# A norm turned by token halves inside the first down stage of a two-block transformer kernel

## The reference

```python
def rms_norm(x, g, eps=NORM_EPS):
    x32 = x.astype(jnp.float32)
    y = x32 * lax.rsqrt(jnp.mean(x32 * x32, axis=-1, keepdims=True) + eps)
    return (y * g.astype(jnp.float32)).astype(x.dtype)

def first_block(x, ...):
    ...                                  # RWKV and differential attention
    hn = rms_norm(h, ln_ffn_pre[l])
    u = causal_dwconv(hn @ w_up[l], conv_w[l], conv_b[l])
    gate, val = jnp.split(u, 2, axis=-1)
    f = (jax.nn.gelu(gate, approximate=True) * val) @ w_down[l]
    h = h + rms_norm(f, ln_ffn_post[l])
    return h

def second_block(x, norm1, w_in, ...):
    h = rms_norm_2(x, norm1[l])
    proj = h @ w_in[l]
    ...
```

## Time and profile before

| | before |
|---|---|
| median of three runs | 2955.22 us (2954.41 to 2957.77) |
| profiled execution | 2959.0 us, span 2957.2 us |
| TensorE busy | 2835.6 us, 96% of the span |
| vector engine busy | 1848.0 us, 62% |
| ScalarE busy | 1269.7 us, 43% |
| GpSimd busy | 623.0 us, 21% |
| mean granted clock of TensorE | 0.989 of 2.4 GHz |

### The profile page before, as it was taken

The page is one execution under the profiler, slowest core; times in us unless marked ns, Lnnn a source line. Parts: engine busy times, 40 slices in busy tenths (PEclk is TensorE's granted clock), DMA queues, the critical chain, the costliest instruction groups (busy, mean ns, idle before and its releaser), DMA issues.

```text
span 2957.2 us, 47458 instructions
## 1 busy us (share of the span) xinstructions
PE 2835.6 (96%) x19678; PEld 2274.4 (77%) x19678; DVE 1848.0 (62%) x2351; ACT 1269.7 (43%) x1879; POOL 623.0 (21%) x313
## 2 busy tenths in 40 slices
PE   8999998889899999999899999999899999999999
PEld 6877777777688888788678867766578888888887
DVE  3157778852599999866685554565645766653446
ACT  4145555542554555443543433343433423333334
POOL 4310122221100000254151200000012122245443
PEclk9999999999999999999999999999899999999999
DMA  6443330002423333465544553435544344465664
GB/s 216 151 121 114 110 131 30 27 26 79 143 89 106 102 101 107 155 220 180 175 133 153 164 178 122 129 112 160 192 150 131 115 150 145 150 216 196 211 238 171
DMA packets 306280, 413.79 MB, mean 140 GB/s; under 512 B 13569, under 2 KB 189834, under 8 KB 306066
## 3 DMA queue, kind: packets, MB, share of 16 engines
q1 hardware_dynamic: 291090, 363.56, 38.6%
q10 hardware_dynamic: 14976, 47.19, 4.2%
HBM read 280.64 MB, written 130.06 MB: 139 GB/s over the span
## 4 chain that ended last, share of the span: by engine, by line
PE 80%; DVE 8%; DMA 4%; issue 3%; ACT 3%; SPq 1%; POOL 1%; DVEq 0%; ACTq 0%; POOLq 0%
PE ps L511 17%; PE ps L2767 16%; PE ps L3300 13%; PE ps L3082 10%; PE ps L2124 5%; PE ps L695 4%; PE ps L1544 4%; PE ps L2175 2%; PE ps L2194 2%; DVE cb L3385 2%; PE ps L2152 1%; PE ps L1607 1%; PE ps L2155 1%; DMA kl<-qk_lo 1%; DMA residual<-src 1%
## 5 line engine op out<-in xcount | busy, mean ns | idle before, releaser
L477 POOL TENSOR_TENSOR wl<-wraw,wh 128x1024 fp32r<-128x1024 f32 x62 | 157.4, 2538 | 1103.0 <-ACT wh L472 1093.4
L511 PE MATMUL ps<-xh,wh 128*128 128x512 f32 x752 | 237.9, 398 | 5.2 <-POOL wl L477 2.3
L511 PE MATMUL ps<-xl,wh 128*128 128x512 f32 x752 | 233.3, 392 | 0.0
L511 PE MATMUL ps<-xh,wl 128*128 128x512 f32 x752 | 232.9, 391 | 0.0
L472 ACT ACTIVATE wh<-wraw 128x1024 fp32r<-128x1024 f32 x78 | 82.4, 1056 | 266.0 <-PE ps L511 205.3
L2756 POOL TENSOR_TENSOR h_dl<-h_dr,h_dh 128x1024 fp32r<-128x1024 f32 x36 | 94.7, 2633 | 477.8 <-ACT h_dh L2738 477.6
L511 PEld LDWEIGHTS ps<-xh,wh 128*128 128x128 f32 x752 | 139.6, 189 | 46.7 <-issue 9.0
L2767 PE MATMUL ps<-h_dh,h_fh 128*128 128x512 f32 x448 | 174.8, 390 | 0.7 <-POOL h_dl L2756 0.7
L2767 PE MATMUL ps<-h_dh,h_fl 128*128 128x512 f32 x448 | 174.4, 389 | 0.0
L2767 PE MATMUL ps<-h_dl,h_fh 128*128 128x512 f32 x448 | 174.3, 389 | 0.0
L511 PEld LDWEIGHTS ps<-xl,wh 128*128 128x128 f32 x752 | 142.4, 189 | 30.3
(11 more groups left out here) (507 smaller groups left out, 7634.6 us busy)
## 6 DMA issues: line engine op xcount, KB each, us to landing
h_fr<-act_d SPq DMA_DIRECT2D x60, 512.0 KB, 3.9
act_d<-act SPq DMA_DIRECT2D x16, 1792.0 KB, 6.7
wraw<-in_w_in SPq DMA_DIRECT2D x48, 512.0 KB, 5.0
...
```

The source lines that it names most:

```text
L477: nc.gpsimd.tensor_tensor(wl[:, s, :, :], wraw[:, s, :, :], wh[:, s, :, :].bitcast(F32), ALU.subtract).then_inc(w_lo, 1)
L511: mm = nc.tensor.matmul(ps[:, bank + h, :], w, x[:, h * HALF:(h + 1) * HALF], start=start and k == 0, stop=stop and k == 2)
```

## The change

1. **Head of the down stage.** ScalarE rounds step 2 before the value tap of the last up tile instead of behind it; the vector engine takes its rest behind the gate taps instead of behind the value taps.
2. **Second half first.** Once P7 is done, tokens 512 to 1023 are complete. Their norm is done while TensorE works on P4: squares and sums among steps 36 and 37, the sum over partitions before block 0 and the spread before block 2 of step 37, then the row work tile by tile on half tiles. Steps 36 to 41 get homes of their own (`last`), outside the second half of `xh` and `xl`, so their loads wait for other things than before.
3. **Last two steps.** The operands of step 40 are rounded behind two norm tiles of the second half, those of step 41 behind three.
4. **After P4** TensorE does the second half of the first two units, with the sums and the spread of the first half's norm between, then the first half of both units with the first half's row work (`first_half_units`).
5. **Next norm's statistics.** The second half's squares are kept in `sq1` and summed between the products; root and reciprocal of that half are made in the middle of the first half's row work, and its spread at tiles 4 and 5.
6. Residual loads and stores are of half tiles; counts of the semaphores follow.

The core of the diff:

```diff
@@ scalar queue
+            down_hi_act(act, down1, 2)
             ff1_tap(act, FF_TILES - 1, "v")
-            down_hi_act(act, down1, 2)
             ff1_gelu(act, FF_TILES - 1)
-            for i in range(3, len(down1.steps)):
+            for i in range(3, LAST1 + 3):
                 down_hi_act(act, down1, i)
...
-            feature_squares_act(act, down1, 24)
-            stat_root_act(act, 3)
-            post_norm_act(act, 1, 16, 32, "norm1_2")
-
-            stat_root_act(act, 4)
+                elif i == LAST1:
+                    root_table_act(act)
+                    for m in range(4):
+                        second_half_squares_act(act, m)
+                        first_half_squares_act(act, m)
+                elif i == LAST1 + 1:
+                    for m in range(4, KT):
+                        second_half_squares_act(act, m)
+            second_half_root_act(act)
+            down_hi_act(act, down1, LAST1 + 3)
+            for kt in (0, 1):
+                second_half_act(act, kt)
+            down_hi_act(act, down1, LAST1 + 4)
+            second_half_act(act, 2)
+            down_hi_act(act, down1, LAST1 + 5)
+            for kt in (3, 4, 5):
+                second_half_act(act, kt)
+            first_half_squares_act(act, 4)
+            second_half_act(act, 6)
+            first_half_squares_act(act, 5)
+            second_half_act(act, 7)
+            for m in (6, 7):
+                first_half_squares_act(act, m)
+            stat_root_act(act, 3, HALF_BANK, FIRST_COLS)
+            post_norm_act(act, 1, 16, 32, "norm1_2", FIRST)
+
+            stat_root_act(act, 4, HALF_BANK, FIRST_COLS)
@@ vector queue
-                    if not more and x == "v":
+                    if not more and x == "g":
                         down_lo_dve(dve, down1, 2)
...
+            second_half_sum_dve(dve, KT - 1)
+            down_prepare_dve(dve, down1, LAST1 + 2)
+            second_half_reciprocal_dve(dve)
+            down_prepare_dve(dve, down1, LAST1 + 3)
+            for kt in (0, 1):
+                second_half_dve(dve, kt)
+            down_prepare_dve(dve, down1, LAST1 + 4)
+            second_half_dve(dve, 2)
+            down_prepare_dve(dve, down1, LAST1 + 5)
+            for kt in (3, 4, 5, 6):
+                second_half_dve(dve, kt)
+            feature_add(dve, down1, "P4", 0)
+            square_sum_dve(dve, 28, FIRST)
+            second_half_dve(dve, 7)
+            feature_add(dve, down1, "P4", 1)
+            square_sum_dve(dve, 29, FIRST)
+            second_half_lo_dve(dve, 7)
+            for b in (2, 3):
                 feature_add(dve, down1, "P4", b)
...
@@ tensor queue
-                down_products(pe, down1, i)
+                down_products(pe, down1, i, {0: second_half_sums_pe, 2: second_half_spread_pe} if i == LAST1 + 1 else {})
             down_last_products(pe, down1)
-            post_sums_pe(pe, 24, KT - 2)
-            spread_pe(pe, 3)
-            paced_units(pe, U_FA, 0, 16, 32, 4)
+            second_half_products(pe, 0, 1, {
+                2: lambda pe: first_half_sums_pe(pe, 24), 3: lambda pe: second_half_square_sums(pe, range(0, 4)),
+                5: first_half_spread_pe, 7: lambda pe: second_half_square_sums(pe, range(4, KT))})
+            second_half_products(pe, 1, 3, {})
+            first_half_units(pe)
@@ sync queue
+                if i == LAST1 + 3:
+                    for kt in (0, 1):
+                        second_half_loads(sp, kt)
+                elif i == LAST1 + 5:
+                    second_half_loads(sp, 2)
                 down_load(sp, down1, i)
...
+            for kt in range(3, KT):
+                second_half_loads(sp, kt)
+            post_norm_loads(sp, 1, FIRST)
@@ new functions
+        def second_half_row_dve(dve, kt):
+            s = kt % 2
+            if kt == 0:
+                h1_pe.wait(dve, "spread", 0)
+            h1_dve.done(nc.vector.tensor_tensor(y[:, kt, SECOND], y[:, kt, SECOND], ps[:, 7, :], ALU.mult), f"m{kt}")
+            h1_dve.wait(dve, f"m{kt}", 0)
+            if kt >= 2:
+                h1_dve.wait(dve, f"l{kt - 2}", 0)
+                h1_act.wait(dve, f"s{kt - 2}", 0)
+            dve.wait_ge(h_loaded[s], 16 * (4 + kt // 2 + 1))
+            dve.wait_ge(src_stored[s], 16 * ((16 + kt) // 2))
+            h1_dve.done(nc.vector.scalar_tensor_tensor(
+                out=src[:, s, SECOND], in0=y[:, kt, SECOND], scalar=col("ln_ffn_post", kt), in1=hres[:, s, SECOND],
+                op0=ALU.mult, op1=ALU.add), f"r{kt}")
+        def second_half_act(act, kt):
+            tile = src[:, kt % 2, SECOND]
+            h1_dve.wait(act, f"r{kt}", 0)
+            h1_act.done(nc.scalar.activation(xh[:, kt, SECOND], tile, ACT.Identity, scale=col("norm1_2", kt)), f"x{kt}")
+            nc.scalar.activation(y[:, kt, SECOND], tile, ACT.Identity, scale=col("norm1_2", kt))
+            h1_act.done(nc.scalar.activation(sq1[:, kt, FIRST], tile, ACT.Square), f"s{kt}")
+            act.dma_start(residual[kt][:, SECOND], tile).then_inc(src_stored[kt % 2], 16)
+        def second_half_products(pe, u, bank, after):
+            for kt in range(KT):
+                h1_dve.wait(pe, f"l{kt}", 0)
+                if kt == 0:
+                    pe.wait_ge(w_lo, U_FA + u + 1)
+                    pe.wait_ge(evac_done, U_FA + u - 1)
+                    pe.wait_ge(down_added, down_added_by(down1, "P4", bank))
+                half_tile(bank, u, kt, SECOND)
+                if kt in after:
+                    after[kt](pe)
+        def first_half_units(pe):
+            for kt in range(KT):
+                first_half_square_sum_pe(pe, 32 + kt)
+                ...
+                mm = half_tile(0, 0, kt, FIRST)
+                if 1 <= kt < KT - 1:
+                    half_tile(2, 1, kt - 1, FIRST)
+                if kt in (4, 5):
+                    next_second_half_spread_pe(pe, kt - 4)
+            mm.then_inc(mm_done, 1)
+            half_tile(2, 1, 6, FIRST)
+            next_first_half_spread_pe(pe)
+            half_tile(2, 1, 7, FIRST).then_inc(mm_done, 1)
```

295 lines of the change are left out of this document (218 added, 77 removed).

## The result

| | before | after |
|---|---|---|
| median, both in the same sessions (20 runs each) | 2957.43 us | 2961.61 us |
| ratio, 95% interval | | 1.0019, 1.0012 to 1.0026 |
| profiled execution / span | 2959.0 / 2957.2 | 2966.96 / 2965.2 |
| mean granted clock in it | 0.989 | 0.987 |

The changed kernel is slower by 0.19%, 5.6 us by the ratio and 4.2 us between the medians; 2950.3 was predicted, with 2957.0 as the upper end. The profiles are single executions: that of after (2966.96) is the second slowest of its 20 runs, so the 8.0 us between the two spans are not what the change costs.

The account below looks back on a forecast made before the run. TensorE, busy 96% of the span, was taken as the bound, so only its idle time could be won: head 2.5 plus tail 2.4 (4.6 - 0.5 - 1.7) made 4.9 us, from 2955.22 to 2950.3, range 2941.5 to 2957.0.

Parts of the forecast that it names:

- The head: Start of the down stage: step 2 begins earlier, the stall moves to step 3; 2.5 us gained after 1.7 clock loss.
- The loads there are released by TensorE, so the gain is kept: Between head and tail of the down stage: nothing there takes back the head's 2.5 us.
- The last two steps: Steps 40 and 41 of the down stage: TensorE, ready at 1436.0, waits 2.9 us for GpSimd's rest at 1438.8.
- the chain of held instructions: Tail: GpSimd's rests hold the vector engine's residual adds, delaying ScalarE's roundings and the last two steps by 2.9 us.
- Third unit at 1483.65 against 1488.26: 4.6 us gained: End of the norm turn after the down stage: third unit starts 4.6 us earlier, before deductions for round trips and clock.
- round trips: Tail: store out and load in of half tiles take 3.5 us, costing 0.15 a tile, 0.5 in the second half.
- 1.7 for the clock: Tail: pauses of 2.9, 2.5 and 3.1 us; first slow stretch hidden, one of the other two counted, 1.7 lost.
- The add of block 1: Tail, vector engine: behind tiles 3 to 7, ends at 1449.6 and frees the bank for the second half's first unit.
- the second pause: Before the second half's first products: TensorE waits 2.5 us for the add of P4 block 1.
- No holding, no clock loss: Rival: roundings of steps 39 to 41 come through and the clock stays full; 12.5 gained, 2942.7 us; chance 0.25.
- Round trips: Rival, tail: half tiles' round trips as long as whole ones', 5.4 us; 6.6 slower, 2961.8 us; chance 0.10.
- The stalls only move: Rival: head gives 1.2, both tail pauses cost slow stretches, half sums cost more; 2955.4 us; chance 0.20.

Follow-up runs that it names:

- e6: The changed kernel with all four P4 adds and squares early and tiles 0 to 4 of both second-half units first on TensorE; 2955.82 us.
- e13: The changed kernel with the four sums of P1's input made ahead of step 5's rest on the vector engine; 2961.83 us.
- e8: The changed kernel with GpSimd's rests from step 38 on cut to 64 of 512 columns, rounded weights multiplied in their place; 2959.24 us.
- e14: The changed kernel with mixed second-half units, deeper head, norm tile 2 behind step 41, and P1's sums ahead of step 5's rest; 2950.41 us.
- e3: The changed kernel with the adds of P4 blocks 0 and 1 and their squares put behind norm tile 4; 2964.48 us.
- e9: The kernel before with the head edit, and the norm's eight residual stores and loads each made as two halves, old order; 2956.20 us.

## Why the prediction was wrong

**The head.** The mechanism was right: step 2 without a pause, 3.40 us before step 3 (3.5). Step 3 came 4.75 us earlier against step 0 (4.2). The term mis-sized was the clock: 1.7 was taken, the window at 1245.47 shows 5.53 us at 0.50, 2.8 lost, as after the longer pause before; that was the lower bound of the range given. The 1.7 did not follow from its own row either: 0.69 over 4.0 us is 1.2 lost. And step 36 stands 1.43 nearer to step 0 (2.5 predicted, bounds 1.2 and 4.2). "The loads there are released by TensorE, so the gain is kept" was wrong as reasoning: the load of step 7 waits for the sums' store. It cost 0.3 in the profile of after and 3.87 in e6, but by e13 nothing in the median. In timed runs the head alone gave nothing (1.0002), so even 1.4 isn't confirmed.

**The last two steps.** P4's end was forecast to 0.2 us of what came, since its cause was: the last two steps began 25.95 us after step 36 (25.85 predicted), right behind GpSimd's rest. The wait was 1.69, not 2.9, because TensorE came there 1.3 later than forecast; the other 2.5 of the 4.2 are mostly the sum and the spreads put into step 37 (0.36 and 1.40 us, and the changes between them). e8 and e14 each take the 1.69 away, the one by shortening GpSimd's rest, the other by putting norm tile 2 behind step 41. So the chain of held instructions was right.

**The step that failed is "Third unit at 1483.65 against 1488.26: 4.6 us gained".** Counted from step 36 this is 4.3 gained (the other 0.3 lay ahead of it); the profile shows 1.7 lost, 6.0 us off. Of these the prediction had set aside 0.5 for round trips and 1.7 for the clock, which made its 2.4 for the tail; measured up to the next ring the tail lost 3.2 against the profile of before. The table gives the parts. (1) The add of block 1 came 1.85 later: five tiles took 2.04 to 2.8 us each where 1.95 stood in the sum; 0.55 and 0.78 of it are waits for round trips, for which 0.5 was taken. (2) 17.65 us instead of 15.6 for the second half's units: 1.5 of it is the clock, at 0.58 for 3.85 us behind the 4.04 us pause, and 0.6 the spread (1.40 instead of 0.8). The prediction had slow stretches behind three pauses, held the first for hidden "by the vector engine" and took one of the other two; the first didn't come, and both others did. This one wasn't hidden, as TensorE had no idle time left to give back until 1488. (3) 14.3 instead of 11.9 for the first half's units up to the last sum: six half tiles at 1.94 instead of 1.71 and one of three products, 1.6 in all, and the two parts of a spread at 0.64 each, where the sum leaves 0.3. The bounds of a half sum (0.28 and 0.57) were meant to cover this, but the sum was 0.35 as taken; it was the products beside it that cost 0.1 each way. The way from there to the third unit took 6.25, 0.3 less than forecast. (4) Behind the third unit came the slow stretch that was taken off: 3.44 us at 0.51, 1.7 lost.

**Deeper than the sizes:** the second pause was put down as a price, 2.5 us, and its cause left alone. e3 and e6 show the cause. TensorE waited for operands that it did not need to want yet; with tiles 0 to 4 of both units first, and the four adds ahead of the last tiles, 5.7 of the 6.0 us come back with no work removed. How much of it the adds and how much the products' order gives isn't shown.

**The rivals.** "No holding, no clock loss" is refuted by the held rows and the windows. "Round trips" gave 2961.8, within 0.2 of the median measured, and that is luck: it has the right sign by the wrong mechanism. The chain of after has two stores on it, of 3.69 and 4.17 us (3.5 was taken, 4.4 was the point from which it decides), the halves' median to landing was 3.6 for loads and 3.8 for stores between 1436 and 1452, and e9, with as many halves in the old order, costs nothing. The Trainium skill, "DMA: Bandwidth & Descriptors", section "Anatomy of one DMA", by which the prediction estimated 3.2 for a half tile that shares the engines, is 0.4 to 0.6 under these medians; and the 3.1 that was called agreement for a whole tile is the shortest of a set whose median is 5.0. Nearest to what happened was "The stalls only move": both pauses cost a slow stretch, and half tiles were dearer on TensorE. It gave 2955.4, and it too lacked the pace of the units and the later add.

These are the chain's pieces around the two (start us, us, what):

```profile
1440.14 3.69 DMA residual<-src
1443.96 0.76 DVE src L2761
1444.75 4.17 DMA residual<-src
```

**What the profiles leave over.** Up to the third unit, after is 0.3 behind before, counted from step 0; at the next ring 1.8; behind the wait for kl, which is 1.9 longer (5.25 against 3.37), 2.9, with a window behind it at 0.50 where before had 0.69. Of the 8.0 us between the spans 1.8 lie ahead of step 0 and 3.3 behind this wait, both within what profiles of one program text differ by. With the new tail this wait was 4.56 to 5.44 in each of ten profiles, with the old one 3.2 to 3.5 in four and 3.99 in e9. The store of qk_lo ahead of it takes 1.2 longer (8.35 against 7.14), but 7.11 in e9. The cause stays open; e14, which has it (4.61), is the fastest kernel, so it decides little.
